# Reordering the two streamed layer norms: where centering, weight casts and small products stand in each engine's order

## The reference

```
def _layer_norm(x, g, b):
    mu = jnp.mean(xf, -1, keepdims=True)
    var = jnp.mean(jnp.square(xf - mu), -1, keepdims=True)
    return ((xf - mu) * lax.rsqrt(var + LN_EPS) * g + b)

x   = _layer_norm(alpha * x   + g1 * y,   ln1_g[i], ln1_b[i])
ctx = _layer_norm(alpha * ctx + cg1 * yc, ln1_g[i], ln1_b[i])
h   = x * (1 + sc2) + sh2     # modulated input of the next stage, likewise for ctx
```

## Time and profile before

| | |
|---|---|
| median of 3 runs | 2397.43 us (2397.41 to 2399.25) |
| the profiled execution | 2398.43 us, span of the trace 2396.6 us |
| TensorE matmul busy | 2306.3 us (96%) |
| VectorE busy | 1698.9 us (71%) |
| ScalarE busy | 1081.3 us (45%) |
| chain that ended last | PE 80%, DVE 12%, ACT 4%, DMA 2%, issue 2% |

### The profile page before, as it was taken

How to read it: one execution, slowest core, us unless ns; L and a number is a source line. 1 busy time by engine, 2 the same in 40 slices (tenths; PEclk the granted TensorE clock), 3 DMA queues, 4 the chain that set the end, 5 groups by cost and what they waited for, 6 DMA issues and landing times.

```text
span 2396.6 us, 41298 instructions
## 1 busy us (share of the span) xinstructions
PE 2306.3 (96%) x17016; PEld 2125.8 (89%) x17016; DVE 1698.9 (71%) x3318; ACT 1081.3 (45%) x1942; POOL 0.2 (0%) x4
## 2 busy tenths in 40 slices
PE   7999999999999999999999999999999999998998
PEld 7869999899999999996999986588888888968997
DVE  6678875678767887577787655466877875377667
ACT  4485444564443544447644532434122234375343
POOL 0000000000000000000000000000000000000000
PEclk9899999999999999988999999999999999999999
DMA  6405665347655566640476532012554522433553
GB/s 223 141 26 195 245 212 190 135 153 252 220 194 178 192 246 219 207 167 22 167 248 219 167 120 74 1 60 99 167 176 158 185 74 94 135 95 110 190 176 123
DMA packets 71098, 374.84 MB, mean 156 GB/s; under 512 B 7424, under 2 KB 17664, under 8 KB 38912
## 3 DMA queue, kind: packets, MB, share of 16 engines
q1 hardware_dynamic: 61456, 361.52, 44.2%
q10 hardware_dynamic: 9456, 10.68, 1.5%
HBM read 369.03 MB, written 1.05 MB: 154 GB/s over the span
## 4 chain that ended last, share of the span: by engine, by line
PE 80%; DVE 12%; ACT 4%; DMA 2%; issue 2%; ACTq 0%; DVEq 0%
PE ps L431 74%; DVE w_lo L1512 5%; DMA w_raw<-weights 2%; PE ps L717 2%; PE ps L700 2%; ACT w_hi L1014 2%; DVE ps L1546 1%; PE ps L657 1%; DVE hid_f L1880 1%; PE ps L646 1%; DVE hid_f L1902 1%; DVE a_lo L1512 1%; ACT a_hi L1037 0%; DVE p_ring L2154 0%; DMA X<-x_t 0%
## 5 line engine op out<-in xcount | busy, mean ns | idle before, releaser
L431 PE MATMUL ps<-a_hi,w_hi 128*128 128x256 f32 (+1 forms) x3184 | 941.7, 296 | 41.3 <-DVE w_lo L1512 20.2
L431 PE MATMUL ps<-a_lo,w_hi 128*128 128x256 f32 (+1 forms) x3184 | 933.0, 293 | 0.0
L431 PE MATMUL ps<-a_hi,w_lo 128*128 128x256 f32 (+1 forms) x3184 | 932.8, 293 | 0.0
L1014 ACT CAST w_hi<-w_raw 128x1024 fp32r<-128x1024 f32 (+1 forms) x628 | 589.2, 987 | 539.5 <-DMA w_raw<-weights 538.7
L1512 DVE TENSOR_TENSOR w_lo<-w_raw,w_hi 128x1024 fp32r<-128x1024 f32 (+1 forms) x632 | 699.3, 1148 | 144.8 <-ACT w_hi L1014 142.3
L431 PEld LDWEIGHTS ps<-a_hi,w_hi 128*128 128x128 f32 x3184 | 613.0, 193 | 61.7 <-issue 36.8
L431 PEld LDWEIGHTS ps<-a_lo,w_hi 128*128 128x128 f32 x3184 | 613.4, 193 | 10.7 <-issue 0.2
L431 PEld LDWEIGHTS ps<-a_hi,w_lo 128*128 128x128 f32 x3184 | 613.0, 193 | 10.8
L431 PE MATMUL ps<-hid_hi,w_hi 128*128 128x256 f32 (+1 forms) x1396 | 431.0, 309 | 7.1 <-DVE w_lo L1512 3.7
L431 PE MATMUL ps<-hid_lo,w_hi 128*128 128x256 f32 (+1 forms) x1396 | 427.7, 306 | 0.0
L431 PE MATMUL ps<-hid_hi,w_lo 128*128 128x256 f32 (+1 forms) x1396 | 427.7, 306 | 0.0
(11 more groups left out here) (200 smaller groups left out, 2053.5 us busy)
## 6 DMA issues: line engine op xcount, KB each, us to landing
w_raw<-weights SPq DMA_DIRECT2D x250, 1024.0 KB, 4.8
pe_sb<-weights SPq DMA_DIRECT2D x96, 512.0 KB, 5.6
w_raw<-weights SPq DMA_DIRECT2D x64, 704.0 KB, 4.0
pe_sb<-na_bias ACTq DMA_DIRECT2D x32, 128.0 KB, 2.1
qk<-qk ACTq DMA_DIRECT2D x8, 256.0 KB, 7.2
X<-x_t SPq DMA_DIRECT2D x1, 1024.0 KB, 7.5
X<-c_rows ACTq DMA_DIRECT2D x2, 512.0 KB, 4.5
qk<-ctx_t ACTq DMA_DIRECT2D x1, 1024.0 KB, 5.8
```

What stands on the lines that cost most here:

```text
L431: return nc.tensor.matmul(out, stationary, moving, start=start, stop=stop)
L1014: nc.scalar.copy(w_hi[:, u % SLOTS, c], raw(u, c)).then_inc(hi_split, 1)
```

## The change

Only the order of instructions is changed, in the two streamed layer norms.

- `shifted` for feature tiles 4 to 7: four instructions of 512 columns become eight of 256. Those of CTX stay in place, those of LAT go two in front of the CTX centering and two into the CTX tile loop.
- Both halves of `w_lo` for the next stage's unit 0 go between the CTX products, behind the second and the third. Before, one stood behind the fourth and one in the CTX tile loop. Those of units 1 and 2 also leave the tile loops and stand between the LAT products.
- ScalarE casts the first of these units behind the first square of the tail (before: behind the third), the second behind the CTX tiles (before: in halves between them), the third between the squares of the LAT products (before: behind them).
- VectorE waits for the mean alone and centers two tiles before the variance, and it centers all eight before the first is normalized.
- The mean and the totals have a hook each. For CTX the hooks are 4 (mean), 6 (totals), 12 (spread) in place of 7, 7, 15. For LAT they are 33, 35, 42 in place of 28, 28, 38.

```
-                hooks = {7: lambda: stream_totals(0), 15: lambda: stream_spread(0)}
+                hooks = {4: lambda: stream_mean(0), 6: lambda: stream_totals(0), 12: lambda: stream_spread(0)}
...
-            layer_hooks = {28: lambda: stream_totals(1), 38: lambda: stream_spread(1)}
+            layer_hooks = {33: lambda: stream_mean(1), 35: lambda: stream_totals(1), 42: lambda: stream_spread(1)}
...
                 for i, q in enumerate(made[0:4]):
                     part_square(4 + i, q)
-                    if i == 2:
+                    if i == 0:
                         split(units[1] + 1)
                 deviation(0)
                 for k in range(KD):
                     modulated(k, CTX, 1)
-                    if k in (5, 7):
-                        split_half(units[1] + 2, (k - 5) // 2)
+                split(units[1] + 2)
                 for i, q in enumerate(made[4:8]):
                     part_square(8 + i, q)
-                split(units[1] + 3)
+                    if i == 1:
+                        split(units[1] + 3)
...
+                def shifted(k, c):
+                    step(v.scalar_tensor_tensor(X[:, k, c], ps[:, STAT, c], -1.0 / (2 * P), X[:, k, c], ALU.mult, ALU.add))
                 for k in range(4, KD):
-                    step(shifted(k))
+                    shifted(k, CTX)
...
                 def stream(s_, beside):
                     tokens = slice(2 * s_, 2 * s_ + 2)
-                    layer_variance(tokens, STREAM_BANKS[s_][1])
+                    dve.wait_ge(ln["mean"], n["chain"] + 1)
                     center(0, s_)
                     center(1, s_)
-                    layer_recip(tokens)
+                    layer_variance(tokens, STREAM_BANKS[s_][1])
                     center(2, s_)
                     center(3, s_)
-                    beside(-1)
+                    layer_recip(tokens)
+                    for k in range(4, KD):
+                        center(k, s_)
                     dve.wait_ge(ln["spread"], n["chain"])
                     sync()
                     for k in range(KD + 1):
                         if k < KD:
-                            if k + 4 < KD:
-                                center(k + 4, s_)
-                            if k == 4:
-                                sync()
                             normalized(k, s_)
...
                 for i, q in enumerate(made[0:4]):
                     arrives(q)
                     counted(4 + i, q)
-                split_half(after, 0)
+                    if i in (1, 2):
+                        split_half(after, i - 1)
+                shifted(4, LAT)
+                shifted(5, LAT)
...
                 stream(0, beside_first)
+                split_half(after + 1, 0)
+                counted(8, made[4])
                 split_half(after + 1, 1)
-                counted(8, made[4])
                 counted(9, made[5])
-                for i in (2, 3):
-                    arrives(made[4 + i])
-                    counted(8 + i, made[4 + i])
+                arrives(made[6])
+                counted(10, made[6])
+                arrives(made[7])
                 split_half(after + 2, 0)
-                stream(1, lambda k: split_half(after + 2, 1) if k == -1 else None)
+                counted(11, made[7])
+                split_half(after + 2, 1)
+                stream(1, lambda k: None)
```

More of the change, by code:

```diff
@@ L564, in shift_mean, with layer_mean, layer_totals @@
                 mm(ps[:, STAT, 0:T], ones, ln_sum[:, 0:T], True, True).then_inc(ln["shift"], 1)
-            def layer_totals(c, mean_bank, tok_bank, many):
+            def layer_mean(c, bank):
                 n["chain"] += 1
+                pe.wait_ge(ln["summed"], n["chain"])
+                mm(ps[:, bank, 0:c.stop - c.start], ones, ln_sum[:, c], True, True).then_inc(ln["mean"], 1)
+            def layer_totals(c, tok_bank, many):
                 n["squares"] += many
[L570 to L573, removed]
+                tokens = range((c.stop - c.start) // P)
                 for j in tokens:
@@ L593, in layer_sums, with stream_mean @@
                 n["ln"] += 1
-                layer_totals(slice(0, T), MEAN, TOK, KD)
+                layer_mean(slice(0, T), MEAN)
+                layer_totals(slice(0, T), TOK, KD)
                 layer_spread(0, T // P, SPREAD, 0)
+            def stream_mean(s_):
+                layer_mean((CTX, LAT)[s_], STREAM_BANKS[s_][0])
             def stream_totals(s_):
-                mean_bank, tok_bank, _ = STREAM_BANKS[s_]
-                layer_totals((CTX, LAT)[s_], mean_bank, tok_bank, (8, 4)[s_])
+                layer_totals((CTX, LAT)[s_], STREAM_BANKS[s_][1], (8, 4)[s_])
             def stream_spread(s_):
@@ L1112, in layer_units @@
                     high_tile(a_hi[:, k, cols], t)
[L1114 to L1119, removed]
             def stream_layer():
@@ L1753, in stream_layer @@
                 n["squares"] += KD + 4
-                _, shifted = layer_begins(res, ALL, 2 * S, r0)
+                layer_begins(res, ALL, 2 * S, r0)
+                def shifted(k, c):
+                    step(v.scalar_tensor_tensor(X[:, k, c], ps[:, STAT, c], -1.0 / (2 * P), X[:, k, c], ALU.mult, ALU.add))
                 for k in range(4, KD):
-                    step(shifted(k))
+                    shifted(k, CTX)
                 sync()
@@ L1817, in stream_layer @@
                     counted(4 + i, q)
-                split_half(after, 0)
+                    if i in (1, 2):
+                        split_half(after, i - 1)
+                shifted(4, LAT)
+                shifted(5, LAT)
                 def beside_first(k):
-                    if k == -1:
+                    if k == 1:
                         arrives(made[4])
-                    if k == 1:
-                        split_half(after, 1)
+                    if k == 2:
+                        shifted(6, LAT)
                     if k == 4:
                         arrives(made[5])
-                    if k == 6:
-                        split_half(after + 1, 0)
+                    if k == 5:
+                        shifted(7, LAT)
                 stream(0, beside_first)
+                split_half(after + 1, 0)
+                counted(8, made[4])
                 split_half(after + 1, 1)
-                counted(8, made[4])
                 counted(9, made[5])
-                for i in (2, 3):
-                    arrives(made[4 + i])
-                    counted(8 + i, made[4 + i])
+                arrives(made[6])
+                counted(10, made[6])
+                arrives(made[7])
                 split_half(after + 2, 0)
-                stream(1, lambda k: split_half(after + 2, 1) if k == -1 else None)
+                counted(11, made[7])
+                split_half(after + 2, 1)
+                stream(1, lambda k: None)
             def add_square():
```

## The result

The changed kernel takes 2404.21 us (median of 19 runs, 2400.53 to 2411.71), the kernel before 2399.02 us in its 19 runs beside it: ratio 1.0021, 95% interval 1.0014 to 1.0028. That is 5.2 us slower. My forecast was 2396.6 and my range ended at 2400.3; to the side on which it came out I had given a chance of 0.03. A second timing on another chip gave 2402.78 against 2399.09 (1.0021, 1.0012 to 1.0030), so the slowdown is no accident of one chip.

The account below looks back on a forecast made before the run. TensorE was taken as the bound (matmuls busy 96%), losing 14.9 us to VectorE waits and the lower clock. First layer norm -0.8, second 0.0, sum -0.8 us: 2396.6 us as a median, range 2393.0 to 2400.3.

Parts of the forecast that it names:

- the replay: VectorE and ScalarE rows re-timed in the new order through the first layer norm, the second assumed alike but for the clock.
- All that was won in the loop but 0.4 us is given back: From last CTX low part to `made[7]`: 5.9 us instead of 4.73; TensorE resumes at 1626.45 against 1626.86.
- list of what would show it: Expected trace signs: waits at mean (2.5 to 3.2 us) and unit 1 (2.8 to 3.6), VectorE and LAT timings, lower clock.
- so the wait itself costs nothing, unless the clock falls: New 2.9 us TensorE wait at the CTX mean: results behind it are taken by VectorE only at 1612.7 and later.
- my second rival: Mean's wait drops the clock too, and the gap at unit 1 at the old price: +2.9 us, 2400.3; chance 0.16.
- The rule of the Trainium skill: Only gaps beyond a certain length throttle TensorE again; both new gaps, 2.9 and 3.2 us, would stay below it.
- half the price of a drop is about 0.7: Tail behind the mean's wait: part of 27 remaining tiles at 1.2 GHz, up to 1.5 us late, in each layer norm.
- 1.2 for the shorter gap of 3.2: Price of a clock drop behind unit 1's wait: 1.2 us, estimated below the 1.57 to 2.35 after 3.9 us.
- -2.0 + 1.2 = -0.8: First layer norm: 2.0 us won at full clock, less 1.2 for a drop at unit 1, net -0.8 us.
- at equal clock the new order is 0.35 us slower: Each layer norm: of the 2.0 us won at full clock, 2.35 were the clock, leaving the order 0.35 slower.
- 1.4 us of the later spread: LAT half: spread hook at 42 for 38, four tiles or 1.4 us later; the LAT loop saves only 0.7.

Follow-up runs that it names:

- a_timed: The changed kernel unaltered, timed again on the same chip as three variants: 2402.78 us, ratio 1.0021 to the kernel before.
- a_lat: Changed kernel with only the LAT products back at 28, 28, 38: 2398.80 us against 2399.07 for before; its repeat 2399.35 (1.0003).
- a_fillmean: Changed kernel with 20 filler matmuls, results never read, ahead of the CTX mean product alone: 2398.65 us against 2399.31 for before (0.9993).
- The square: Changed kernel with neither, either or both of CTX products at 13, 14, 20 and LAT at 28, 28, 38, one chip: 2402.78, 2399.81, 2399.35, 2395.59 us.
- b_fill: Kernel before with 24 filler matmuls, results never read, ahead of unit 1 only: 2395.72 us against 2398.62 for before (0.9985).
- a_fill: Changed kernel with 20 filler matmuls each ahead of the CTX mean product and ahead of unit 1: 2395.67 us against 2398.62 for before (0.9986).
- a_fill_early: Changed kernel with fillers at both waits and LAT products at 20, 20, 30: 2392.64 us against 2399.07 for before (0.9975).
- b_fill_early: Kernel before with 24 fillers ahead of unit 1 and LAT products at 20, 20, 30: 2391.59 us against 2399.31 for before (0.9966).
- a_hooks: Changed kernel with all hooks as before (CTX 7, 7, 15; LAT 28, 28, 38): 2398.66 us against 2398.62 for before (1.0002).
- a_late_lat: Changed kernel with CTX products at 13, 14, 20 and LAT products at 28, 28, 38: 2395.59 us, ratio 0.9984 to before.
- after_again: The changed kernel unaltered, run once more for its clock: 2401.63 us in one execution.
- a_late: Changed kernel with CTX products at 13, 14, 20, LAT late: 2399.71 us against 2398.62 for before (1.0002); repeat a_late_2 2399.81 (0.9997).
- b_hooks: Kernel before with only the changed hooks (CTX 4, 6, 12; LAT 33, 35, 42): 2407.42 us against 2399.31 for before (1.0032).

## Why the prediction was wrong

**Right: the replay.** All steps of VectorE from the shifts to unit 1 came within 0.2 us in the first layer norm, and both new waits within 0.3 us in both. "All that was won in the loop but 0.4 us is given back" is 30.26 against 29.95 on the ruler. Of the list of what would show it, all seven entries came true (last CTX low part 23.45 us behind the shifts for 23.35, LAT tiles at a distance of 0.94 us, as forecast). A replay that is right in every listed entry still missed the time, because no entry spoke of the clock behind the mean's wait.

**The step that failed first** is "so the wait itself costs nothing, unless the clock falls". The fall had a case of its own, my second rival, with a chance of 0.16. In the traces with this wait of 2.7 us (after, a_timed, the repeated run of after, and a_lat with its repeat) the clock fell behind it in 8 of 10 layer norms. I had it as less likely than not from one length of 1.55 that held and one of 3.9 that didn't, while 2.7 lies between. The rule of the Trainium skill that I had quoted ("TensorE: Matmul & The Clock Gate", section "HAM oscillation — how this bites in real kernels") would have had both new gaps harmless; these rows decide against it. That the fall is the cause, and not the time waited or the order, a_fillmean shows: there TensorE spends the same time on fillers.

**Its price was wrong as well.** The rival had "half the price of a drop is about 0.7" for each layer norm, as if only the end of the tail came later. What comes late is the totals and the spread, since six tiles and both small products between them run at the lower level; VectorE's chain (variance, spread, loop, `made[7]`) hangs on them and passes the whole delay to unit 1. After's second layer norm: spread 2.95 us later (7.24 for 4.29), unit 1 3.08 us later (33.03 for 29.95). The square has 3.0 and 3.8 us for taking the wait away.

**The second step** is the clock behind unit 1. I took "1.2 for the shorter gap of 3.2". The clock fell behind 2.94 us as behind 3.9. What a fall costs is the longer way from unit 1 to the LAT mean against a kernel with fillers and the products at the same places (4.75 us in b_fill, 6.54 in a_fill): 2.3 and 1.5 us in before, 2.6 and 1.5 in after. Over all traces it is 1.3 to 2.6 behind gaps of 3.6 to 3.9 us and 1.4 to 2.6 behind gaps near 2.9 where the clock fell. Shortening a gap that still drops the clock wins only its own length. So "-2.0 + 1.2 = -0.8" for the first layer norm became +0.76 (52.42 less 51.66): at full clock -1.9 (a_fill, 49.78), and the drop cost 2.6 in the place of 1.2.

**Right as a net, and not seen as two parts,** was "at equal clock the new order is 0.35 us slower". With the clock held it is 0.40 (a_fill 49.78, b_fill 49.38). But this is a gain with a larger cost inside. With the clock down behind unit 1 alike, five products later are 1.88 us at the LAT mean (39.03 against 37.15), of which the LAT loop gives back 0.38 (13.32 for 13.70), so 1.50 stays in each layer norm; the rest of the new order saves 1.1, which a_fill_early against b_fill_early bears out with 1.0. I had the 1.4 us of the later spread on paper and didn't ask what the change would be without it.

The sum by the ruler, against before: first layer norm +1.81 at the LAT mean, -1.05 in the loop; second -0.30 to unit 1 with the clock held, +3.08 for its fall, +1.79 from there to the LAT mean, -1.05 in the loop. Together +4.3, where the span has +3.9 and the last low part of the second layer norm 4.1. The forecast had -0.8: 1.6 of the difference is the second step, 3.1 the first, 0.4 the second step again in the second layer norm. The medians differ by 5.2 and 3.7 on two chips; what lies between these two is not explained.

**What stays open.** Why the clock fell behind the same wait in one layer norm and held in another was not found. The square leaves the split of the loss as two parts of 3 to 4 us each; a difference of two such medians is uncertain by 2 to 3 us, so neither is called the larger. And a_hooks, with the LAT products at 28, 28, 38 and a wait of 1.64 us at the mean, is level with before, while a_late_lat, as short on the ruler, is 3.5 us faster. Whether a fall behind the 1.64 us in more of the executions makes that difference was not tested.

## What to carry to other kernels

When an engine with a clock that falls gets a new wait, price the work behind the wait at the lower level up to where another engine's chain takes it over, not only the wait; and give the fall a chance by the lengths that were seen to drop it. A small product on which a chain of fixed length hangs sets the end of its stage by its place: move it as early as its inputs allow, and read from the chain's last row, not from the waits, what it costs to be late. If a stage has several edits that are each level with the old kernel, time them together on one chip before calling any the cause.

## What the runs showed of the hardware

Of waits of one length some drop the clock and some don't. Waits of TensorE over 1.5 us from the start of the shifts on, in the two layer norms of all 18 traces:

| wait, us | clock fell | where |
|---|---|---|
| 3.25 to 3.9 | 16 of 16 | ahead of unit 1 |
| 2.92 to 2.97 | 8 of 9 | ahead of unit 1 (held in a_lat, second layer norm) |
| 2.7 | 8 of 10 | at the mean |
| 2.45 | 0 of 1 | ahead of unit 1, after_again |
| 2.13 | 2 of 2 | ahead of unit 1, a_late and its repeat |
| 1.95 | 2 of 6 | ahead of unit 0, a_late, its repeat and a_late_lat |
| 1.62, 1.64 | 1 of 5 | a_hooks, b_hooks, b_fill_early |
| 1.55 | 0 of 5 | ahead of unit 0, before, b_fill, b_fill_early |

A fall behind 1.95 us, a_late_2:

```profile
1984.50 0.36 PE L431 MATMUL ps<-a_hi,w_hi 128*128 128x256 f32 x1 [1.95 <-DVE X L1766]
1984.69 0.36 PE L431 MATMUL ps<-a_lo,w_hi 128*128 128x256 f32 x1
1984.85 0.41 PE L431 MATMUL ps<-a_hi,w_lo 128*128 128x256 f32 x1
```

The third matmul takes 0.41 us where 0.28 is usual, and so the lower level begins here within 0.4 us of the wait's end. It can begin later too: in the first layer norm of a_timed the granted clock is 1.00 in the 2 us behind the mean's wait and 0.51 in the next 2. In these cases a fall is not bound to a length, but is likelier behind a longer wait. And 20 to 24 matmuls whose results nobody reads, in waits of 2.7 to 3.9 us, kept the clock at full in every layer norm in which they stood at both waits or in the old order (four kernels, eight of eight), and behind the mean's wait in both layer norms of a_fillmean; b_fill won 2.9 us by them.
